# A step-ahead state space, two more projected blocks in front of z, and a shorter routing that issues its first gathers

## The chip, the cores and the metric

One core of one Trainium2 chip runs the whole program in one launch. The metric is the device time of that core in microseconds (us). The kernel before was timed three times: 1570.29, 1573.99 and 1575.91 us, median 1573.99. The engines are TensorE (PE; its weight loads are PEld), VectorE (DVE), ScalarE (ACT), GpSimd (POOL) and SyncE (SP), which here only issues DMAs.

## The reference

512 tokens of width 1024 pass through two transformer blocks, all in float32. Block 1, cut to what the change touches:

```python
proj = x @ w_in                          # q k v iq ik iw z xbc dt
q, k, iq, ik = rope(q), rope(k), rope(iq), rope(ik)
att = dsa_attention(q, k, v, iq, ik, iw) # index scores pick 128 keys a query, then softmax
xbc = silu(conv4(xbc)); dt = softplus(dt_raw + dt_bias)
y   = ssd_chunked(xs * dt, dt * a, B, C) # 4 chunks of 128 tokens, 8 heads, state 64x64
y   = rms((y + d_skip * xs) * silu(z)) * norm_w
x   = layer_norm(ALPHA * x + [att, y] @ w_out)
x   = layer_norm(ALPHA * x + moe(x))     # 16 experts in 4 groups, 2 of a token's best group
```

Inside `ssd_chunked`, a chunk gives three things: a diagonal part (C B^T masked by decays, times X), the chunk's own contribution to the state, and C times the state carried in from the chunks before. Block 2 has two other attention branches and a second `moe` with 32 experts, 2 a token. In both `moe`s a token's rows are gathered by expert, each expert has its own weights (3 MB), and the two results of a token are added with gates.

## The kernel before, in words

A product in "three passes" (L238 to L242) writes a float32 operand as a high part that the PE multiplies fast and a low remainder, and adds high x high, low x high and high x low. The high part is an ACT copy and the low one a subtraction on POOL. A projected block of 128 columns is 8 pieces (one for each 128 rows of `w_in`) of three matmuls over all 512 tokens.

`front` (L347) projects blocks in the order FIRST (ten), each turned by rope or convolved, then z in 8 steps over 4 token tiles. At its start POOL alone makes the low part of the first weight (L514) and of all eight pieces of x (L526). After the tenth block DVE has 16 rounds of top-k (L366 to L369: MAX8 and MATCH_REPLACE8) for two of the query tiles.

`state_space` (L903) works the four chunks and, between their steps, the five blocks of LATER (40 pieces, L240 to L242 with `ssd_main`). The order of each engine is written out by hand. PE's order a chunk is: products (L978, L984, after DVE took the chunk before), states (L990), segments (L999), pieces, diagonals (L1008), a rotation (L970). DVE per chunk: inputs X and Xd (L1174, L1175), masked products (L1178), the state (L1188 to L1199), skip (L1205), two masks MT (L1211), the carried part (L1216, L1218), then y (L1220, L1222). POOL: cumulated decays (L1059), low parts (L1064), and the three operations of rope (L1069 to L1074). After the last chunk come the four roots on ACT (L1161) and four normalisations on DVE (L1233, L1234).

`route` (L1769) turns the router's logits into lists: for each tile of an expert (96 rows in block 1, 64 in block 2) which tokens are in it. It is one long chain of small DVE instructions, each of which waits for the one before (`step`), with three places where PE sums or gathers (L1823, L1824, L1829). The SP queue meanwhile loads the first experts' weights. The next code block, `experts` (L1951) or `experts_moving` (L2213), blanks the two gather buffers on DVE (L2163, L2459), copies an index column (L2052, L2339) and gathers the first tile's rows with an indirect DMA from POOL (L2055, L2342). PE's first transpose and SP's next weight load (L1765, called with the slots `late`) wait for that gather's semaphore `x_in[0]`.

Between code blocks all engines meet at a barrier, which is how a stage's last engine sets the start of the next.

## Time and profile before

| what | us |
|---|---|
| median of three runs | 1573.99 |
| the profiled execution, its own time | 1573.33 |
| its span in the trace | 1571.2 |
| PE busy over the span | 1297.1 |
| DVE, ACT, POOL busy | 714.0, 447.4, 440.1 |

The profile page gives shares over the whole span, and the stages differ: where PE is nearly always busy in one, it stands still for most of another. So the table of stretches (busy time of each engine between two times, granted PE clock, DMA share) is the view to begin with, and then the instructions in order of time at the borders of the stages. A granted clock of 1.00 is 2.4 GHz and 0.50 is 1.2 GHz. Busy times of PE overlap a little from one matmul to the next, so the distance between two starts is the better price.

### The profile page before, as it was taken

The page shows a single profiled execution, that of the slowest core. Times are in us where ns is not written, and L with a number is a line of the kernel's source. Part 1 is how long each engine was busy: PE and PEld are TensorE (multiplying, and loading weights), DVE is VectorE, ACT ScalarE, POOL GpSimd, SP SyncE. Part 2 cuts the span into 40 slices and gives each one's busy share as a digit, 9 for nine tenths or more (in the row PEclk, how much of TensorE's full clock was granted, in tenths as well). Part 3 has the DMA queues.
Part 4 walks back from the last instruction along what each step waited for, and adds up shares of the span by engine and source line. Part 5 has one row for each costly group of instructions (what it writes and reads, how often), then busy time and mean ns, then how long its engine had stood idle before and what let it go on. Part 6 is the DMA issues. An engine that isn't in the chain of part 4 may idle for free. (4 is left out here: it accounts for less than half of the span.)

```text
span 1571.2 us, 20768 instructions
## 1 busy us (share of the span) xinstructions
PE 1297.1 (83%) x7632; PEld 1047.4 (67%) x7634; DVE 714.0 (45%) x1283; ACT 447.4 (28%) x964; POOL 440.1 (28%) x418
## 2 busy tenths in 40 slices
PE   6968789939999419889999999999798929977782
PEld 5757467838999319768989978788676815544441
DVE  2797684553443464753653637672233351111112
ACT  3532322213332124433342243423323201111110
POOL 6336410201110204202423324134244003322223
PEclk9989968958999758989999999999899859999996
DMA  6200170149996431300311312322131589999995
GB/s 252 96 3 12 71 251 30 41 175 354 384 372 249 133 115 49 132 1 6 107 68 68 107 46 91 110 81 81 36 104 52 215 319 375 385 385 392 400 361 179
DMA packets 64699, 262.71 MB, mean 167 GB/s; under 512 B 8276, under 2 KB 18132, under 8 KB 51808
## 3 DMA queue, kind: packets, MB, share of 16 engines
q1 hardware_dynamic: 53600, 234.25, 40.0%
q0 software_dynamic: 9216, 20.99, 4.1%
q10 hardware_dynamic: 1792, 6.29, 1.1%
q8 instruction: 53, 0.87, 0.2%
q14 instruction: 38, 0.31, 0.1%
HBM read 242.56 MB, written 29.43 MB: 173 GB/s over the span
## 5 line engine op out<-in xcount | busy, mean ns | idle before, releaser
L1693 POOL TENSOR_TENSOR block_w_lo<-block_w,block_w_hi 128x512 fp32r<-128x512 f32 x96 | 130.4, 1360 | 220.7 <-ACT block_w_hi L1671 220.7
L2377 PE MATMUL e_gu<-e_w,e_xT 128*64 128x256 f32 x1024 | 129.9, 411 | 35.5 <-DMA e_w<-in_gu 34.6
L2377 PEld LDWEIGHTS e_gu<-e_w,e_xT 128*64 128x64 f32 x1024 | 84.1, 148 | 72.0 <-issue 42.1
L240 PE MATMUL dil_bank<-block_w_hi,xT_hi 128*128 128x512 f32 x288 | 116.8, 406 | 4.3 <-PEq L768 4.3
L241 PE MATMUL dil_bank<-block_w_lo,xT_hi 128*128 128x512 f32 x288 | 114.9, 399 | 0.0
L242 PE MATMUL dil_bank<-block_w_hi,xT_lo 128*128 128x512 f32 x288 | 114.8, 399 | 0.0
L1671 ACT ACTIVATE block_w_hi<-block_w 128x512 fp32r<-128x512 f32 x96 | 60.4, 631 | 182.8 <-PE dil_bank L242 117.4
L2447 DVE TENSOR_TENSOR e_prod<-e_sg,e_gu 128x128 f32<-128x128 f32 x32 | 9.2, 288 | 165.1 <-ACT e_sg L2487 165.1
L240 PEld LDWEIGHTS dil_bank<-block_w_hi,xT_hi 128*128 128x128 f32 x288 | 77.6, 269 | 8.6 <-issue 4.7
L241 PEld LDWEIGHTS dil_bank<-block_w_lo,xT_hi 128*128 128x128 f32 x288 | 77.7, 270 | 4.1
L242 PEld LDWEIGHTS dil_bank<-block_w_hi,xT_lo 128*128 128x128 f32 x288 | 77.6, 269 | 4.2
L778 POOL TENSOR_TENSOR block_w_lo<-block_w,block_w_hi 128x512 fp32r<-128x512 f32 x20 | 24.8, 1270 | 157.6 <-ACT block_w_hi L851 157.6
L2950 DVE COPY dil_nat<-dil_bank 128x512 f32<-128x512 f32 x36 | 24.9, 691 | 87.2 <-PE dil_bank L242 85.9
L2401 PE MATMUL e_ybank<-e_w,e_hT 128*64 128x512 f32 x256 | 62.2, 604 | 0.4 <-issue 0.4
L2084 PE MATMUL e_gate<-e_xT,e_w 128*128 128x96 f32 x512 | 61.7, 280 | 0.7 <-DVE e_xT L2132 0.7
L2084 PEld LDWEIGHTS e_gate<-e_xT,e_w 128*128 128x128 f32 x512 | 60.3, 197 | 1.0 <-issue 1.0
L2084 PEld LDWEIGHTS e_up<-e_xT,e_w 128*128 128x128 f32 x512 | 59.5, 192 | 1.7
L2084 PE MATMUL e_up<-e_xT,e_w 128*128 128x96 f32 x512 | 59.3, 274 | 0.0
L260 PE MATMUL hT_bank<-consts,h_nat 128*128 128x128 f32 x32 | 6.2, 383 | 55.6 <-PEq L1543 55.6
L2487 ACT ACTIVATE e_sg<-e_gu 128x128 f32<-128x128 f32 x32 | 8.9, 277 | 150.9 <-PE e_gu L2377 150.9
L2146 DVE TENSOR_TENSOR xT_lo<-e_w,xT_hi 128x2048 fp32r<-128x2048 f32 x16 | 36.7, 2292 | 33.1 <-ACT xT_hi L2199 31.3
L240 PE MATMUL gates_bank<-block_w_hi,xT_hi 128*128 128x512 f32 x128 | 50.5, 395 | 1.0 <-PEq L768 1.0
(477 smaller groups left out, 3154.4 us busy)
## 6 DMA issues: line engine op xcount, KB each, us to landing
e_w<-in_gu SPq DMA_DIRECT2D x48, 2048.0 KB, 16.3
e_w<-in_dn SPq DMA_DIRECT2D x48, 1024.0 KB, 18.6
block_w<-in_w_dil SPq DMA_DIRECT2D x9, 2048.0 KB, 8.1
block_w<-in_w_out SPq DMA_DIRECT2D x4, 2048.0 KB, 8.9
block_w<-in_w_gates SPq DMA_DIRECT2D x4, 2048.0 KB, 11.1
slot_rows<-blank SPq DMA_DIRECT2D x12, 512.0 KB, 5.9
slot_rows<-e_y ACTq DMA_DIRECT2D x16, 384.0 KB
w_t<-in_w_in_t SPq DMA_DIRECT2D x10, 512.0 KB, 3.9
```

Of the source, the lines that this page charges most:

```text
L240: pe.matmul(out, lhs[0], rhs[0], start=first, stop=False)
L241: pe.matmul(out, lhs[0], rhs[1], start=False, stop=False)
L242: return pe.matmul(out, lhs[1], rhs[0], start=False, stop=last)
L778: pool.tensor_tensor(lo, w, hi.bitcast(F32), ALU.subtract)
L1671: act.activation(wh[:, j % RING, 0:width[i]], k.w[:, slot, c, 0:width[i]], ACT.Copy).then_inc(hi_ready, 1)
L1693: pool.tensor_tensor(wl[:, j % RING, 0:width[i]], k.w[:, (q0 + i) % 2, c, 0:width[i]], wh[:, j % RING, 0:width[i]].bitcast(F32), ALU.subtr ...
L2084: ins = pe.matmul(bank[b % 2][:, m * S:(m + 1) * S], w1[b][:, w:w + P], xT[b % 2][:, c * S:(c + 1) * S], start=(c == 0), stop=(c == KD - 1))
L2146: dve.tensor_tensor(w2_part(k.xl, b, 0), w2[b][:].rearrange("p (q n) -> p q n", q=4), w2_part(k.xh, b, 0).bitcast(F32), ALU.subtract).then ...
L2377: ins = pe.matmul(gubank[b % 2][g * S:(g + 1) * S, 0:2 * FG], xT[b % 2][:, c * S:(c + 1) * S], w1[b][:, w:w + 2 * FG], start=(c == 0), sto ...
L2401: ins = pe.matmul(bank[rows_of, :], hT[:, c * S:(c + 1) * S], w2[b][:, c * DM + m * 512:c * DM + (m + 1) * 512], start=(c == 0), stop=(c = ...
L2447: dve.tensor_tensor(prod[:], sg[:], gubank[b % 2][0:U, FG:2 * FG], ALU.mult).then_inc(prod_ready, 1)
L2950: return dve.tensor_copy(nat[:, i, tt, :], bank[:, 0:512])
```

## The change

In `front`, blocks 4 and 0 move from LATER to FIRST, so twelve blocks are projected in front of z and three remain in the state space. Their rope is done there by ACT and POOL (`late_rope`) between z's steps. At the start, the low part of the first weight and of the odd pieces of x is made on DVE, the rest on POOL.

In `state_space`, the diagonal, states and products are put in another order: DVE makes the next chunk's inputs and masked products before it takes the y of this chunk, PE computes the next chunk's products while this one's diagonals run, and the carried part is read earlier. The squares of three chunks get one root and one reciprocal, and the last its own. The SP load of the fifth block goes.

In `route`, pairs of DVE instructions are joined, ranks over token tiles are summed by PE in bfloat16 (eight matmuls), the thresholds (5 in block 1, 7 in block 2) are compared in one instruction with a sum behind it, the gates are moved behind the list of tokens, and the first half of the gathering matmuls may start a token choice earlier. POOL blanks the gather buffers in `route` and issues the first two gathers there as soon as `tok_of` is written; the experts' block then starts at the third.

```diff
-FIRST = (14, 7, 5, 6, 8, 9, 10, 11, 12, 13)
-LATER = (4, 0, 1, 2, 3)
+FIRST = (14, 7, 5, 6, 8, 9, 10, 11, 12, 13, 4, 0)
+LATER = (1, 2, 3)
@@ front
+                def late_rope(i):
+                    r = ROPED + i
+                    o = k.ropeT[:, FIRST[LATE0 + i], :]
+                    pool.wait_ge(raw_ready, r + 1)
+                    pool.tensor_tensor(o, raw[:, r % 2, :], k.c("cos"), ALU.mult).then_inc(cos_done, 1)
+                    pool.wait_ge(turn_ready, i + 1)
+                    pool.tensor_tensor(relu[:, r % 2, :], relu[:, r % 2, :], k.c("sin"), ALU.mult).then_inc(sin_done, 1)
...
-                split_w(0)
-                for c in range(KD):
+                for c in range(0, KD, 2):
                     pool.wait_ge(xh_ready, c + 1)
...
+                dve.wait_ge(wh_ready, 1)
+                dve.tensor_tensor(w_l[:, 0], w_t[:, 0], w_h[:, 0].bitcast(F32), ALU.subtract).then_inc(first_low, 1)
+                for c in range(1, KD, 2):
+                    dve.wait_ge(xh_ready, c + 1)
+                    dve.tensor_tensor(k.xl[:, c], xT[:, c], k.xh[:, c].bitcast(F32), ALU.subtract).then_inc(xl_ready[1], 1)
@@ state_space, PE's order from the first chunk to the third
                 products(0)
+                states(0)
                 segment(0)
                 segment(1)
                 pieces(0, 4)
+                products(1)
+                pieces(4, 5)
                 diagonal(0)
-                pieces(4, 8)
+                pieces(5, 6)
                 diagonal(1)
-                products(1)
                 segment(2)
-                rotate(0)
-                pieces(8, 10)
                 segment(3)
+                states(1)
+                pieces(6, 8)
+                products(2)
...
@@ state_space, DVE
+                inputs(0)
+                masked(0)
                 for c in range(TT):
                     if c < TT - 1:
+                        state(c)
...
+                    if c < TT - 1:
+                        inputs(c + 1)
+                        masked(c + 1)
...
                     dve.wait_ge(ydiag_done, 2 * (c + 1))
                     dve.tensor_tensor(y2[:], y1[:], b_y[:], ALU.add).then_inc(y_free, 1)
@@ route
+                for x in k.xg:
+                    pool.memset(x[:], 0.0).then_inc(xg_ready, 1)
+                pool.wait_ge(k.rows_stored, 16 * TT)
+                pool.wait_ge(xg_ready, 2)
+                pool.wait_ge(tok_ready, 1)
+                for b in range(2):
+                    pool.indirect_dma_start(k.xg[b][:], None, rows, bass.IndirectOffsetOnAxis(
+                        ap=k.tok_of[:, b:b + 1], axis=0), bounds_check=SEQ - 1, oob_is_err=False).then_inc(x_in[b], 16)
...
+                for tt in range(TT):
+                    pe.matmul(totals[:, 0:E], ones[:], M[:, tt, :], start=(tt == 0), stop=(tt == TT - 1))
+                pe.matmul(rbank[:, 0:TT * E], before[:], flat, start=True, stop=False)
+                for tt in range(1, TT):
+                    ins = pe.matmul(rbank[:, tt * E:TT * E], ones[:], flat[:, 0:(TT - tt) * E], start=False, stop=(tt == TT - 1))
...
+                step(dve.tensor_tensor(above[:], bc(totals[:, 0:E], 2, J), bc(full[:], 1, E), ALU.is_gt))
+                step(dve.reduce_sum(extra[:], above[:], AX))
@@ experts, experts_moving
-                for x in xg:
-                    dve.memset(x[:], 0.0).then_inc(blank, 1)
```

## Rows read from the trace of the kernel before

**Rows 1.** Stretches: length, busy us (instructions) by engine, PEclk, DMA share, GB/s.
```profile
20.50:105.00 84.50, 84.40 (x376) 64.97 (x376) 64.14 (x122) 38.69 (x68) 35.70 (x19) 1.00 0.27 94
...
116.30:187.20 70.90, 55.78 (x298) 44.45 (x298) 48.45 (x67) 21.43 (x37) 45.74 (x28) 0.93 0.03 8
187.20:327.20 140.00, 125.67 (x654) 99.19 (x656) 81.98 (x155) 38.63 (x102) 20.20 (x16) 0.82 0.32 114
...
355.40:520.00 164.60, 163.81 (x1294) 151.82 (x1295) 66.04 (x90) 54.01 (x67) 16.26 (x28) 0.98 0.86 326
...
1288.80:1535.00 246.20, 210.59 (x1521) 119.92 (x1521) 31.46 (x94) 40.05 (x94) 69.71 (x119) 0.94 0.99 378
```
**Rows 2.** Order of time (start, us, engine, line) at the start of `front`.
```profile
5.82 2.34 POOL L514 TENSOR_TENSOR w_t_lo<-w_t,w_t_hi 128x1024 fp32r<-128x1024 f32 x1 [5.38 <-ACT w_t_hi L544]
9.35 8.80 POOL L526 TENSOR_TENSOR xT_lo<-block_w,xT_hi 128x512 fp32r<-128x512 f32 x7
20.53 0.50 PE L240 MATMUL proj_main<-xT_hi,w_t_hi 128*128 128x512 f32 x1 [1.35 <-POOL w_t_lo L514]
```
**Rows 3.** Order of time, a projection's matmuls and the end of `front`.
```profile
21.33 0.39 PE L240 MATMUL proj_main<-xT_hi,w_t_hi 128*128 128x512 f32 x1
21.56 0.40 PE L241 MATMUL proj_main<-xT_lo,w_t_hi 128*128 128x512 f32 x1
...
102.90 2.66 ACT L627 ACTIVATE z<-proj_main 128x512 f32<-128x512 f32 x4
...
115.14 0.69 DVE L373 TENSOR_SCALAR key_bias<-score 128x256 bf16<-128x256 f32 x2
```
**Rows 4.** DVE groups by line in 116.3 to 187.2: busy us, mean ns, idle before.
```profile
L1211 DVE TENSOR_TENSOR ssd_mt<-ssd_l,ssd_gm 128x512 f32<-128x512 f32 x8 | 13.1, 1664 | 0.8 <-ACT ssd_l L1101 0.6
L1220 DVE TENSOR_TENSOR ssd_y<-ssd_y,ssd_ydiag 128x512 f32<-128x512 f32 x4 | 2.7, 687 | 9.7 <-PE ssd_ydiag L1008 9.7
L1233 DVE RECIPROCAL ssd_ms<-ssd_ms 128x1 f32<-128x1 f32 x4 | 0.7, 163 | 5.1 <-ACT ssd_ms L1161 5.0
```
**Rows 5.** Order of time in the second chunk, and the stage's last instruction.
```profile
137.16 2.82 POOL L1064 TENSOR_TENSOR block_w_lo<-block_w,block_w_hi 128x1024 fp32r<-128x1024 f32 x1
137.78 4.20 DVE L1211 TENSOR_TENSOR ssd_mt<-ssd_l,ssd_gm 128x512 f32<-128x512 f32 x2
177.13 1.29 POOL L1074 TENSOR_TENSOR ropeT<-ropeT,x_res 128x512 f32<-128x512 f32 x1
185.96 0.75 DVE L1234 SCALAR_TENSOR_TENSOR ssd_y<-ssd_y,ssd_ms,ssd_vec 128x512 f32<-128x512 f32 x1
```
**Rows 6.** Order of time in block 1's `route`.
```profile
335.66 0.80 DVE L1896 SCALAR_TENSOR_TENSOR r_extra<-r_counts,r_extra 128x16 f32<-128x16 f32 x4
340.61 0.56 DVE L1917 TENSOR_TENSOR r_ohr<-consts,r_r 128x384 f32<-128x384 f32 x1
343.01 2.76 PE L1829 MATMUL r_tbank<-r_ohj,r_ohr 128*96 128x26 f32 x16 [9.72 <-DVE r_ohj L1920]
345.89 0.18 DVE L1933 TENSOR_SCALAR r_tok_of<-r_tbank 96x26 uint32<-96x26 f32 x1 [1.59 <-PE r_tbank L1829]
```
**Rows 7.** Order of time, block 1's first gather and the weight load behind it.
```profile
351.08 1.16 POOL L2055 DMA_INDIRECT e_xg<-token_rows,e_idx  x1 [1.02 <-issue]
355.38 0.34 SPq L1765 DMA_DIRECT2D e_w<-in_gu  x1
```
**Rows 8.** Landing of the 48 gathers; DMA in two stretches.
```profile
DMA to landing us min/median/max: 3.8/10.5/12.0
...
344.00:348.00 4.00, 1.78 (x12) 1.65 (x11) 0.70 (x4) 0.00 (x0) 0.00 (x0) 0.50 0.04 16
...
1284.00:1286.00 2.00, 0.00 (x0) 0.00 (x0) 0.45 (x1) 0.00 (x0) 0.48 (x2) 0.50 0.71 295
```
**Rows 9.** Order of time, block 2's token list and its next load.
```profile
1280.08 0.20 DVE L1933 TENSOR_SCALAR r_tok_of<-r_tbank 64x48 uint32<-64x48 f32 x1
1288.77 0.33 SPq L1765 DMA_DIRECT2D e_w<-in_gu  x1
```

More of the change, by code:

```diff
@@ L351, in front @@
     NB, CONV0 = len(FIRST), 1 + ROPED
+    LATE0 = CONV0 + CONV_BLOCKS
     TAKEN, FLOOR, ROUNDS = -3.0e38, -1.0e35, TOPK // 8
@@ L1130, in square, with roots @@
                         act.wait_ge(squared, c)
-                    act.activation(yy[:], k.y[:, c, :], ACT.Square, accum_out=ms[:, c, 2:3]).then_inc(squared, 1)
+                    act.activation(yy[:], k.y[:, c, :], ACT.Square, accum_out=ms[:, 0, c:c + 1]).then_inc(squared, 1)
+                def roots(first, end):
+                    act.activation(ms[:, 2, first:end], ms[:, 1, first:end], ACT.Sqrt).then_inc(rms_ready, 1)
                 split_high(0)
@@ new lines, in state @@
+                def state(c):
+                    dve.wait_ge(st_done, c + 1)
+                    s3 = St[:].rearrange("p (h d) -> p h d", h=4)
+                    if c >= 1:
+                        for g in range(2):
+                            r = slice(HD * g, HD * (g + 1))
+                            step(dve.tensor_tensor(s3[r], s3[r], bc(decay[r, 1, c * 8 + 4 * g:c * 8 + 4 * g + 4], 2, HD),
+                                                   ALU.mult))
+                    for g in range(2):
+                        r = slice(HD * g, HD * (g + 1))
+                        if c >= 1:
+                            ins = dve.tensor_tensor(St[r, :], St[r, :], b_st[r, g * HW:(g + 1) * HW], ALU.add)
+                        else:
+                            ins = dve.tensor_copy(St[r, :], b_st[r, g * HW:(g + 1) * HW])
+                        if g == 0:
+                            step(ins)
+                    ins.then_inc(st_ready, 1)
@@ L1782, in route @@
     k.exp_of = k.sb(ctx, f"{name}_exp_of", [1, NT - E], I32)
+    k.xg = [k.sb(ctx, f"{name}_xg{i}", [S, DM]) for i in range(2)]
     k.used = k.sb(ctx, f"{name}_used", [1, 1], I32)
@@ L1792, in route @@
         picked = k.sb(s, f"{name}_picked", [P, 2, TT, E])
-        M = k.sb(s, f"{name}_m", [P, TT, E])
-        extra, cum, base, zero, counts = (k.sb(s, f"{name}_{n}", [P, E]) for n in ("extra", "cum", "base", "zero",
-                                                                                  "counts"))
-        rank = k.sb(s, f"{name}_rank", [P, TT, E])
+        M, ones, before = (k.sb(s, f"{name}_{n}", shape, BF16) for n, shape in (("m", [P, TT, E]), ("ones", [P, P]),
+                                                                              ("before", [P, P])))
+        full = k.sb(s, f"{name}_full", [P, J])
+        above = k.sb(s, f"{name}_above", [P, E, J])
+        past = k.sb(s, f"{name}_past", [P, 2, TT, J])
+        extra, cum, base, zero = (k.sb(s, f"{name}_{n}", [P, E]) for n in ("extra", "cum", "base", "zero"))
         cmp = k.sb(s, f"{name}_cmp", [1, NT - E, E])
@@ L1834, in _ @@
             def _(act):
+                act.activation(ones[:], k.c("ones"), ACT.Copy).then_inc(bits_ready, 1)
+                act.activation(before[:], k.c("before"), ACT.Copy).then_inc(bits_ready, 1)
+                act.activation(full[:], k.c("iota")[:, 1:J + 1], ACT.Copy, scale=float(S)).then_inc(bits_ready, 1)
                 act.wait_ge(diff_ready, 1)
@@ L1904, in _ @@
                 step(dve.reduce_sum(tile[:], picked[:], AX))
-                step(dve.tensor_scalar(over[:], pos[:], S - 0.5, None, ALU.is_gt))
-                q_now = over
-                for j in range(2, -(-SEQ // S)):
-                    step(dve.scalar_tensor_tensor(q[:], pos[:], j * S - 0.5, q_now[:], ALU.is_gt, ALU.add))
-                    q_now = q
+                step(dve.tensor_tensor(past[:].rearrange("p i t j -> p (i t) j"), bc(pos[:].rearrange("p i t -> p (i t)"), 2, J),
+                                       bc(full[:], 1, 2 * TT), ALU.is_ge))
@@ L1911, in _ @@
+                step(dve.reduce_sum(q[:], past[:], AX))
+                step(dve.tensor_scalar(over[:], q[:], 1.0, None, ALU.min))
                 step(dve.tensor_tensor(tile[:], tile[:], own[:], ALU.subtract))
                 step(dve.tensor_tensor(tile[:], tile[:], over[:], ALU.mult))
+                step(dve.tensor_tensor(own[:], own[:], q[:], ALU.add))
                 step(dve.tensor_tensor(tile[:], tile[:], own[:], ALU.add))
-                step(dve.tensor_tensor(tile[:], tile[:], q[:], ALU.add))
@@ L1959, in experts @@
     with ExitStack() as s:
-        xg = [k.sb(s, f"{name}_xg{i}", [S, DM]) for i in range(2)]
+        xg = k.xg
         idx = [k.sb(s, f"{name}_idx{i}", [S, 1], U32) for i in range(2)]
@@ L2226, in experts_moving @@
     with ExitStack() as s:
-        xg = [k.sb(s, f"{name}_xg{i}", [S, DM]) for i in range(2)]
+        xg = k.xg
         idx = [k.sb(s, f"{name}_idx{i}", [S, 1], U32) for i in range(2)]
```

365 lines of the change are left out of this document (176 added, 189 removed).

## The prediction

> **What bounds the kernel now.** I read the table of stretches first. It shows three kinds of stage that the change touches [rows 1]. From 20.5 to 105 PE is busy 84.4 of 84.5 us: that part of `front` is PE's. From 116.3 to 187.2 (the state space) PE has 55.8 of 70.9, DVE 48.5 and POOL 45.7: three engines share the bound, so a gain on one is cut short by the next. The experts of block 1 are PE's (163.8 of 164.6), those of block 2 are the DMA's (share 0.99 over 246 us). Both shift rigidly with the moment at which they begin, and they begin with the landing of a gather. Second, the order of time at the four borders: the start of `front` [rows 2], its end [rows 3], the list of tokens [rows 6] and the first gather [rows 7, 9]. Third, the groups of the state space [rows 4, 5], where the idle time before an instruction and its mean against its shortest say who waits.
>
> **Start of `front`.** POOL starts the first low part of w at 5.82 and takes 2.34, then eight pieces of x at 8.80/7 = 1.26, then the second w; PE can start its second block at 20.53 and waited 1.35 for it [rows 2]. In the new code DVE makes the first w: two halves of about 0.6 (a DVE operation of 512 columns is recorded with 0.69 [rows 4]), done at 7.0. The x pieces alternate, four of 1.26 on POOL and four of 0.69 on DVE. Do they run beside each other? The masks MT say no: two that should take 1.4 took 4.20 while POOL had a 2.82 us subtraction and another after it [rows 5]. So the eight pieces take 4 x 1.95 = 7.8, to 14.8; POOL's second w takes 2.34, to 17.2. PE's first block keeps up with this (its last piece comes at 14.8 and takes 0.7). The start comes 3.3 earlier (2 if ACT's high parts are late, 5 if the two engines do not block each other).
>
> The Trainium skill, page SBUF — State Buffer, "Who interferes with whom", says that a DVE instruction with two SBUF inputs and a GpSimd one that reads SBUF exclude each other for a whole instruction. The row above agrees. Had it not held, the x pieces would end at 12.0 and the start would come 5 earlier.
>
> **Rest of `front`.** PE gets 2 blocks x 24 matmuls x 0.23 (start to start in [rows 3]) = 11.1, and two rotations, which I price with their neighbours at 1.5 together (0.9 to 2.5; no row of mine shows one alone). The last silu of z ended at 102.90 + 2.66 = 105.56 [rows 3]. It now ends at 105.56 - 3.3 + 12.6 = 114.9. DVE's top-k rounds set the end before: 115.14 + 0.69 = 115.83 [rows 3]; they move with the start, to 112.5. So this stage gains only 0.9: DVE had covered 10.3 us of PE's idle time and the two new blocks fill it. ACT and POOL have room: both are busy under half of the stretch [rows 1], and POOL's six new rope operations (1.29 each [rows 5]) lie between low parts of z that PE needs every 2.8 us (12 x 0.23). Range of the stage: 2 lost to 2 gained. DMAs: the same blocks load, one SP issue less later; no queue is passed.
>
> **State space.** Removed: 16 pieces, 16 x 0.70 = 11.2 of PE, two rotations, two low parts (2.34) and six rope operations on POOL: its work falls from 8 x 1.0 + 5 x 2.34 + 15 x 1.29 = 39 to 26.6. DVE loses no work but waits: the eight MTs cost 1.664 on average against 0.69, so 7.8 us are blocked time [rows 4]; with two thirds of POOL's work left some 2.6 of these go, and about as much on its other two-input operations. DVE also stood 9.7 before L1220 (it waits for the diagonals) and 5.1 before the roots came back [rows 4]. The new order puts the next chunk's inputs into the first, and one root for three chunks ahead of the last y shortens the second to 1 or 2.
>
> To join these I walked both written orders, each engine taking its next instruction when its semaphores allow it, with the durations of the trace and DVE's two-input operations and POOL's excluding each other. For the order of before it gives 71.1; measured are 186.71 - 116.3 = 70.4 [rows 5]. For the new order DVE's y2 of the four chunks comes at 13.7, 26.4, 40.4 and 48.9 and the last POOL rope at 57.4, DVE at 56.2. **I take 57.4, a gain of 13.4** (rounded down from 13.7). Bounds: 50 if POOL hardly blocks (DVE 48.5 less 5, plus its first waits), 62 if each chunk keeps DVE's chain of 12.4 (the present period of 14.3 less 1.6 of waiting and its gaps) and the clock costs 2. What is late next is POOL: it ends the stage with three ropes behind one another. PE now idles up to 3.8 us at a time; its clock is at 0.93 in this stage [rows 1].
>
> **Route, block 1.** A small dependent step costs 0.80/4 = 0.20 [rows 6]. From the ranks to the first `ohr` the chain ran to 340.61. New chain: ranks are ready about 333.6 (eight bfloat16 matmuls for four float32 entries; 333.3 to 334.3), thresholds and their sum 0.55, scan and base 0.44, four instructions of 128 columns 1.28, `past` and its sum 0.44, eight small ones 1.6: 337.9. Two choices of 0.3 + 0.3 + 0.56 [rows 6]: 340.2. PE's first half runs under the second choice, so its second half, 1.4 of 2.76 [rows 6], ends at 341.7, and `tok_of` at 341.9 against 345.89 + 0.18 = 346.07: 4.2 earlier. The six gate steps (1.2) move behind it and delay nothing that the gather needs. Then the gather itself: before, 5.0 lay between `tok_of` and the issue at 351.08 (barrier, two blankings, an index copy), 4.30 from issue to SP's next load [rows 7]. Now the issue follows in about 1.0 (its own "issue" time in [rows 7]), at 342.9; landing at 347.2. POOL's second issue ends about 345.9 and the barrier costs 1.5, so the experts start at 347.4 against 355.4. **Gain 8.0.** The weights have landed by then: DMA share is 0.04 from 344 [rows 8]. POOL's blanking and semaphore clears have 14 us of cover; without it at most 3. Bounds 5 to 10.
>
> **Route, block 2.** Same counts with 32 experts: I get 1276.2 for `tok_of` against 1280.28 [rows 9]; issue at 1277.1. But here three experts' weights are still arriving, to about 1285.3 (share 0.71 in 1284 to 1286 [rows 8]). Gathers took 3.8 to 12.0, median 10.5 [rows 8], so this one lands between 1281 and 1287. The stage behind is DMA-bound, so what counts is only the gap between 1285.3 and 1288.8, the load that SP issues at the landing [rows 9]: 3.5 at most, 1.5 at least. I take **2.5**.
>
> The Trainium skill, page DMA: Bandwidth & Descriptors, "SWDGE vs HWDGE vs iDMA", says that each DMA engine goes round its queues in turn, hardware and software ones. By that a gather is not held until the weights are in, and the gain is the whole gap, 3.5; the median of 10.5 speaks for less. It moves the sum by 1.
>
> **Sum.** 0.9 + 13.4 + 8.0 + 2.5 = 24.8. Against the profiled execution's own 1573.33 that is 1548.5; it lies within 1 us of the median of the runs, so no correction.
>
> **Rivals.**
> *Gathers wait for the queue.* Issued into running weight loads they land 12 us later instead of 4.3 [rows 8]: block 1 then starts at 354.9 and gains 0.5, block 2 gains 0. Sum 14.8: 1558.5. Against it: block 1's loads end at 344.
> *DVE's chain stays the bound of the state space* at 62 or more, and `front` ends 1 later: gain 8 - 1 + 10.5 = 17.5, 1556.
> *More than forecast:* the state space at 53, whole gap in block 2, a warmer PE in the stages behind (187 to 327 ran at 0.82 [rows 1]): 31, 1542.
> *Slower than before:* PE has 55.8 - 11.2 - 2 = 43 us of work in a stage of 57, and long pauses bring the clock to 0.5, as in 344 to 348 [rows 8]. If it stays there for the whole stage the work is 86 us, 28 more than the forecast's 57.4: 24.8 of gain turn into a loss of 3.8, 1577. It decides from 25 us of added PE time. Against: most of its pauses are under 4 us.
> *The change does not do what it says:* order and waits leave the stages as they were, 1573, within 0.3%.
>
> **Chances.** Forecast 0.62 (its own range 1543 to 1554), queue 0.10, chain 0.13, more 0.08, slower 0.03, nothing 0.04. The range 1540 to 1561 leaves out under 2 in 10. This kernel's runs lie 5.6 apart, so 0.3% (4.7 us) is about what can be told from no change. Faster 0.93, same 0.04, slower 0.03.
>
> **What would show it.** PE's second block starts near 17.2; z's last silu and not a top-k round ends `front`, near 115; the state space lasts 55 to 60 and its last instruction is POOL's rope; MT's mean falls below 1.4; the first indirect DMA starts near 343 in block 1 and near 1277 in block 2, and both stand before the barrier; the experts' stages last as long as before. I am wrong if an expert stage lengthens by what its start gains, or if the clock row of the state space falls well under 0.93.

## The result, and the profile after

The changed kernel takes 1554.86 us (median of four runs, 1552.74 to 1559.26), the kernel before 1574.87. The ratio is 0.9894, 95% interval 0.9860 to 0.9928: faster by 11 to 22 us. The forecast was 1548.5 in a range of 1540 to 1561. The profiled execution of the changed kernel is its slowest, 1559.26 with a span of 1557.2.

First the table of stretches of the changed kernel: length, busy us (instructions) of PE, PEld, DVE, ACT and POOL, PEclk, DMA share, GB/s. It answers to [rows 1].

```profile
16.10:105.00 88.90, 88.90 (x390) 68.35 (x389) 68.09 (x134) 41.02 (x67) 46.79 (x27) 1.00 0.28 98
114.40:176.40 62.00, 47.01 (x246) 37.11 (x246) 46.65 (x63) 16.84 (x29) 29.59 (x20) 0.87 0.00 1
176.40:315.80 139.40, 122.79 (x656) 96.77 (x656) 81.69 (x155) 38.63 (x102) 20.19 (x16) 0.84 0.32 114
337.90:502.50 164.60, 163.90 (x1290) 151.90 (x1291) 66.15 (x90) 53.41 (x66) 16.24 (x28) 0.98 0.87 325
1275.00:1520.60 245.60, 211.03 (x1521) 119.37 (x1523) 31.22 (x94) 39.70 (x94) 69.54 (x118) 0.94 0.99 378
```

The state space went from 70.9 to 62.0. The stages that the change does not touch kept their lengths (139.4, 164.6, 245.6). One stretch differs that the table shows only in part: from block 1's first expert tile to block 2's route it took 904.2 before and 907.8 after. But for the place of the first two gathers, its code is the same in all 13 kernels profiled here, and its length follows the mean granted clock in it, from 907.8 at 0.925 (the changed kernel) to 894.0 at 0.941 (e6). That is why the stages below are compared, and not only the totals.

The table gives, for every kernel of this study, what its profile says of the stages. "No drain" means that the barrier at the end of `route` does not wait for GpSimd's own DMAs (e1). State space: first `ssd_go` matmul to attention's first. Tile 1 and tile 2: start of the first transpose of an expert's tile (`e_xbank`) behind the route's first instruction (`r_zero`), block 1 and block 2. MB: what the DMAs moved in the first 60 us of block 2's route (its GB/s times 60). Last: start of PE's last group of `e_gu` matmuls behind block 2's route start. The ratio stands to the kernel before on the same chip; the chips differ (the kernel before took 1565.3 beside e11 and 1574.9 beside the changed kernel), so totals are to be compared by the ratio and not by the median.

| kernel | state space | tile 1 | tile 2 | MB | last | median us | ratio (95%) |
|---|---|---|---|---|---|---|---|
| before | 70.9 | 28.2 | 29.2 | 21.6 | 275.3 | 1574.9 | |
| after | 62.0 | 22.0 | 29.3 | 21.5 | 274.9 | 1554.9 | 0.9894 (0.9860 to 0.9928) |
| e1 no drain | 60.8 | 19.3 | 25.9 | 22.4 | 272.4 | 1548.5 | 0.9853 (0.9822 to 0.9883) |
| e2 gathers back | 61.8 | 24.3 | 28.6 | 21.7 | 275.2 | 1553.0 | 0.9881 (0.9848 to 0.9913) |
| e3 route only | 70.9 | 22.2 | 29.1 | 21.8 | 275.3 | 1569.8 | 0.9986 (0.9965 to 1.0007) |
| e4 front, state space | 63.0 | 28.0 | 29.1 | 21.6 | 274.2 | 1559.1 | 0.9915 (0.9881 to 0.9949) |
| e5 warm | 57.8 | 22.0 | 28.9 | 21.8 | 274.4 | 1551.1 | 0.9879 (0.9841 to 0.9918) |
| e6 states early | 56.4 | 22.0 | 29.0 | 21.8 | 274.6 | 1547.1 | 0.9858 (0.9820 to 0.9895) |
| e7 four slots, no drain | 62.4 | 19.5 | 20.3 | 22.0 | 273.9 | 1547.2 | 0.9850 (0.9811 to 0.9889) |
| e8 gather between loads | 62.0 | 19.5 | 26.0 | 22.2 | 273.6 | 1551.7 | 0.9879 (0.9838 to 0.9920) |
| e9 no drain, states early | 55.4 | 19.4 | 25.8 | 22.5 | 272.1 | 1544.5 | 0.9830 (0.9795 to 0.9865) |
| e10 all three | 56.0 | 19.4 | 26.0 | 22.4 | 273.0 | 1542.9 | 0.9830 (0.9787 to 0.9872) |
| e11 six slots | 62.1 | 22.2 | 29.2 | 21.6 | 274.4 | 1547.8 | 0.9881 (0.9847 to 0.9914) |

**Front.** Order of time in the changed kernel (start, us, engine, line, operation, tiles), as in [rows 2, 3]:

```profile
5.74 1.22 DVE L708 TENSOR_TENSOR w_t_lo<-w_t,w_t_hi 128x1024 fp32r<-128x1024 f32 x1 [4.59 <-ACT w_t_hi L575]
7.11 6.67 DVE L711 TENSOR_TENSOR xT_lo<-block_w,xT_hi 128x512 fp32r<-128x512 f32 x4
...
13.19 2.84 POOL L531 TENSOR_TENSOR w_t_lo<-w_t,w_t_hi 128x1024 fp32r<-128x1024 f32 x1
...
111.00 0.69 DVE L374 TENSOR_SCALAR key_bias<-score 128x256 bf16<-128x256 f32 x2
...
111.47 2.66 ACT L666 ACTIVATE z<-proj_main 128x512 f32<-128x512 f32 x4
```

POOL's second low part ends at 16.03 (forecast 17.2), z's last silu at 114.13, behind the last top-k round at 111.69. The state space starts at 114.43 against 116.37: 1.9 us.

**State space.** DVE's groups (busy us, mean ns, idle before), as in [rows 4]:

```profile
L1268 DVE TENSOR_TENSOR ssd_mt<-ssd_l,ssd_gm 128x512 f32<-128x512 f32 x8 | 8.8, 1132 | 1.6 <-ACT ssd_l L1140 1.5
...
L1227 DVE TENSOR_TENSOR ssd_state<-ssd_state,ssd_decay 64x256 f32<-64x256 f32 x4 | 4.1, 1022 | 3.5 <-PE ssd_st L1032 3.4
...
L1277 DVE TENSOR_TENSOR ssd_y<-ssd_y,ssd_ydiag 128x512 f32<-128x512 f32 x4 | 2.8, 688 | 5.6 <-PE ssd_ydiag L1050 5.6
```

The masks fell from 1.664 to 1.132 on average, the wait for the diagonals from 9.7 to 5.6, the one for the roots from 5.0 to nothing. New is a wait of 3.4 for `states` (L1032). The longest wait of PE's matmuls there (engine, line, releaser: us in total, times, longest):

```profile
PE ssd_go L1019 <- DVE ssd_y L1256: 6.7, 2, 4.1
```

A stand is a time in which PE has nothing to do. It has three here: 2.6 us up to 117.50, 2.6 up to 136.8, and 4.1 up to 153.4. PE's granted clock about them is the third number from the end:

```profile
117.00:120.00 3.00, 2.50 (x7) 2.14 (x8) 1.32 (x4) 0.71 (x1) 2.65 (x1) 0.50 0.02 5
120.00:123.00 3.00, 3.00 (x16) 3.00 (x15) 2.06 (x4) 0.60 (x1) 1.04 (x1) 0.50 0.00 0
135.00:138.00 3.00, 1.18 (x8) 0.89 (x8) 2.87 (x5) 1.67 (x3) 1.84 (x1) 0.82 0.00 0
138.00:141.00 3.00, 3.00 (x11) 1.89 (x8) 2.96 (x3) 0.00 (x0) 2.22 (x2) 0.61 0.00 0
153.00:156.00 3.00, 2.63 (x12) 1.82 (x13) 2.90 (x5) 0.00 (x0) 0.00 (x0) 0.66 0.00 0
156.00:159.00 3.00, 3.00 (x17) 2.56 (x15) 1.18 (x3) 0.60 (x1) 0.94 (x1) 0.77 0.00 0
```

0.50 is the 1.2 GHz level, 1.00 the 2.4 GHz one. From 123 to 135 and from 141 to 153 the clock is 0.99 and 1.00 on average.

**Routes.** Order of time in both, as in [rows 6, 7, 9]:

```profile
329.41 0.18 DVE L1989 TENSOR_SCALAR r_tok_of<-r_tbank 96x26 uint32<-96x26 f32 x1 [0.51 <-PE r_tbank L1901]
...
330.63 1.14 POOL L1882 DMA_INDIRECT r_xg<-token_rows,r_tok_of  x1 [10.19 <-issue]
332.07 0.96 POOL L1882 DMA_INDIRECT r_xg<-token_rows,r_tok_of  x1 [0.31 <-issue]
...
337.55 0.34 SPq L1820 DMA_DIRECT2D e_w<-in_gu  x1
...
1262.36 1.01 POOL L1882 DMA_INDIRECT r_xg<-token_rows,r_tok_of  x1 [9.69 <-DVE r_tok_of L1989]
1263.67 0.95 POOL L1882 DMA_INDIRECT r_xg<-token_rows,r_tok_of  x1 [0.30 <-issue]
...
1274.64 0.33 SPq L1820 DMA_DIRECT2D e_w<-in_gu  x1
...
1275.01 1.08 PE L2424 MATMUL e_xbank<-consts,r_xg 64*128 64x64 f32 x8 [14.73 <-PEq L1866]
```

In block 1 the first gather is issued 14.7 us behind the route's start in place of 23.8, 9.0 earlier, but SP's next load comes only 6.4 earlier (PE's first tile 6.2): 6.9 us lie between issue and load, where before it were 4.3 [rows 7]. In block 2 the issue is 9.3 earlier (16.7 against 26.0) and the experts start at 29.3 against 29.2: nothing. PE's wait there is not for a DMA but for L1866, which is `with nc.Block() as block` of `route`: its closing barrier. DVE had done its last at 1263.30 and POOL its second issue at 1264.62.

### The profile page after: what moved, and what is told of

It is laid out like the page before. It is cut to its first block and busy times, and to the rows that moved or that the text cites. A ratio compares the mean times of both kernels' runs of the same rounds, so it can differ in the third digit from the quotient of the medians.

```text
span 1557.2 us, 20719 instructions
## 1 busy us (share of the span) xinstructions
PE 1300.1 (83%) x7642; PEld 1049.4 (67%) x7642; DVE 710.7 (46%) x1248; ACT 448.6 (29%) x968; POOL 430.3 (28%) x413
## 5 line engine op out<-in xcount | busy, mean ns | idle before, releaser
L822 POOL TENSOR_TENSOR block_w_lo<-block_w,block_w_hi 128x512 fp32r<-128x512 f32 x20 | 24.8, 1272 | 155.9 <-ACT block_w_hi L895 155.9
L2144 PEld LDWEIGHTS e_gate<-e_xT,e_w 128*128 128x128 f32 x512 | 60.8, 198 | 1.0 <-issue 1.0
L2768 POOL TENSOR_TENSOR block_w_lo<-block_w,block_w_hi 128x384 fp32r<-128x384 f32 (+2 forms) x28 | 29.2, 1048 | 79.6 <-ACT block_w_hi L2781 79.6
## 6 DMA issues: line engine op xcount, KB each, us to landing
e_w<-in_gu SPq DMA_DIRECT2D x48, 2048.0 KB, 14.7
```

The source lines that it names most:

```text
L822: pool.tensor_tensor(lo, w, hi.bitcast(F32), ALU.subtract)
L2144: ins = pe.matmul(bank[b % 2][:, m * S:(m + 1) * S], w1[b][:, w:w + P], xT[b % 2][:, c * S:(c + 1) * S], start=(c == 0), stop=(c == KD - 1))
L2768: pool.tensor_tensor(wl[:, j % RING, 0:width[i]], k.w[:, (first_chunk + i) % 2, c, 0:width[i]], wh[:, j % RING, 0:width[i]].bitcast(F32), ...
```

## The experiments

**e1: the closing barrier.** What does the barrier wait for? The DMA records of the changed kernel point at the two gathers. The last packets of the software queue, which here carries GpSimd's gathers, end at 336.00 in block 1 and at 1273.11 in block 2, and SP's next loads come 1.5 us behind each, at 337.55 and 1274.64. So the wait for GpSimd's own DMAs, the drain, is taken out of the barrier, in `route` alone:

```diff
-        with nc.Block() as block:
+        with nc.Block(no_gpsimd_drain=True) as block:
```

> The changed kernel, with one edit in route: its block closes without waiting until GpSimd's own DMAs are done (no_gpsimd_drain=True), everything else stays. In the changed kernel SP loaded again only at 337.55 and TensorE turned its first tile at 337.89, although the second gather was issued at 333.03 and no DMA moved data after 336. Theory A, the closing barrier waits for both gathers to end: without it, block 1's route ends some 1.5 us after the second issue (about 334.5), TensorE then waits for the first gather alone and starts 1.5 to 2.5 us earlier (335.5 to 336.5, where the route starts at 315.8); in block 2 the engines leave the block at about 1266 in place of 1274.5 and wait for the first gather itself, which the weight queue holds up: 0 to 1.5 us there. Together 1.5 to 4 us less. Theory B, the gathers' own landing sets both starts: engines leave the block earlier, but SP's load and TensorE's first transpose stay 21.8 and 13.8 us behind the route's start: 0 us.

Order of time in this kernel, both routes, and its DMAs in the first 60 us of block 2's route:

```profile
327.58 1.14 POOL L1882 DMA_INDIRECT r_xg<-token_rows,r_tok_of  x1 [10.17 <-issue]
...
332.18 1.51 PE L2135 MATMUL e_xbank<-consts,r_xg 96*128 96x96 f32 x8 [5.92 <-DMA r_xg<-token_rows,r_tok_of]
...
1253.20 1.01 POOL L1882 DMA_INDIRECT r_xg<-token_rows,r_tok_of  x1 [9.70 <-DVE r_tok_of L1989]
...
1262.43 1.08 PE L2424 MATMUL e_xbank<-consts,r_xg 64*128 64x64 f32 x8 [11.30 <-DMA r_xg<-token_rows,r_tok_of]
...
1236.50:1296.50 60.00, 36.00 (x285) 21.58 (x285) 20.80 (x79) 9.01 (x21) 14.02 (x22) 0.73 0.98 374
```

PE now waits for the gather by name, and SP loads again at 1262.31, before the gathers' last packet at 1264.06. Block 1 starts 4.6 us behind the issue in place of 7.3 (2.7 less), block 2 9.2 in place of 12.7 (3.4 less). Theory A, and by more than its numbers (1.5 to 2.5 in block 1, 0 to 1.5 in block 2). By stages the barrier had cost 5.2 us: 2.7 in block 1 and 2.5 at the last group of block 2. The median is 6.3 lower, 1548.54, but in the profiles 1.2 of that is a state space of 60.8 in place of 62.0, which the edit does not touch, and the intervals of the two ratios overlap a little.

**e2: the early issue alone.** The first two gathers and the blanking of their tiles go back to the experts' block (the short routing stays):

```diff
 route:
-                for x in k.xg:
-                    pool.memset(x[:], 0.0).then_inc(xg_ready, 1)
...
-                for b in range(2):
-                    pool.indirect_dma_start(k.xg[b][:], ...).then_inc(x_in[b], 16)
 experts, now for the first two tiles as well:
                     pool.tensor_copy(idx[b % 2][:], k.tok_of[:, bass.ds(t, 1)]).then_inc(idx_ready, 1)
...
+                for x in xg:
+                    dve.memset(x[:], 0.0).then_inc(blank, 1)
```

> The changed kernel with the first two gathers (index copy, issue) and the blanking of their tiles back in the experts' block, as before; the shorter routing stays. Prices the early issue alone. Theory A (the gathers inside route are worth the code between tok_of and the issue, less what the closing barrier now waits for): block 1's experts start 3 to 4 us later than in the changed kernel (about 341 for a route start at 315.8), block 2's 1 to 3 us later: 4 to 7 us more in all. Theory B (the barrier gives all of it back): under 1.5 us more. Block 2: if its gather is held by the weights' queue alone, an issue some 9 us later still lands behind the same weights, and its start moves by less than 2 us.

Order of time, block 2:

```profile
1263.87 1.03 POOL L2396 DMA_INDIRECT e_xg<-token_rows,e_idx  x1 [0.92 <-POOL e_idx L2393]
...
1270.20 1.09 PE L2422 MATMUL e_xbank<-consts,e_xg 64*128 64x64 f32 x8 [14.00 <-DMA e_xg<-token_rows,e_idx]
```

Block 1 starts 2.3 later than in the changed kernel. Block 2, issued 5.6 us later, starts 0.7 earlier: 6.3 us from issue to use. Block 2's last group comes 0.3 later. So by stages the early issue is worth 2.6 us, between theory B (under 1.5) and theory A (4 to 7), and the total shows nothing of it (ratio 0.9881 against 0.9894). It is nearer to theory B: the barrier gives most of it back. In block 1, 3.9 of the 6.2 us that the route won are thus the shorter chain, and 2.3 the early gathers.

**e3 and e4: the parts apart.** e3 is the kernel before with the new `route` and experts; e4 the kernel before with the new `front` and `state_space`:

```diff
 e3: -def route(k, name, E, G, S, lg, ctx, loads, retired):
     +def route(k, name, E, G, S, lg, ctx, loads, retired, rows, x_in):      # and what it holds; front, state_space of before
 e4: +                inputs(0)                                              # and all of front and state_space; route of before
     +                masked(0)
```

> The kernel before with the change's part in route and the experts alone; front and state space as before. By the two traces the routes gave 6.4 us in block 1 and 0.1 in block 2: theory A (parts add up) 6.5 us less than before, so about 1568. The forecast's 10.5 us for both routes would give 1564. If the gain hangs on the earlier parts (clock of later stages, other order), under 4 us.

> The kernel before with the change's part in the front and the state space alone; route and experts as before. By the two traces the front gave 2.0 us and the state space 8.9, attention 0.6: theory A (parts add up) 11 us less than before, about 1563.5; the forecast had 14.3 us for both. If the clock in stages behind takes some back, 7 to 10 us.

By stages the parts stand as in the whole: e3 has a tile 1 of 22.2 and a tile 2 of 29.1, e4 a state space of 63.0. By time e4 is 13.2 us under the kernel before (expected were 11). e3 is only 2.4 under it; by its interval it is between 5.5 us faster and 1.1 slower, which leaves out the expected 6.5. How much of this is the clock can be seen in runs of equal mean clock. At 0.903 and 0.904 e3 took 1567.2 to 1568.7 and the kernel before 1569.6 to 1573.2, some 3 us more, and e4 took 1558.1 to 1561.8, some 11 us less than the kernel before. So e4 is theory A, and of e3's 4 missing us the clock explains about 1. The other 3 or so stay open: e3's tile 1 comes 6.0 earlier in its profile, and no view shows where that is lost.

**e5: keep PE busy.** 36 bfloat16 matmuls, whose result is overwritten, in the three places where PE stands, the last of them behind a new wait for `turn_ready`:

```diff
                 products(0)
+                keep_warm(10)
                 states(0)
...
+                keep_warm(10)
                 products(2)
...
+                pe.wait_ge(turn_ready, 1)
+                keep_warm(16)
                 products(3)
```

> The changed kernel with 36 extra bfloat16 matmuls (128 x 512, into a bank whose result is overwritten later) in the state space, in the places where TensorE stands: 10 behind products(0), 10 ahead of products(2), 16 ahead of products(3). In the changed kernel its stands of 2.6, 2.6 and 4.1 us stood beside a granted clock of 0.50 in 117 to 123, 0.61 to 0.82 in 135 to 141 and 0.66 to 0.77 in 153 to 159. Theory A (the clock lost there is the reason why the state space took 62.0 us and not 57.4): with no stand the granted clock stays near 1.00 and the stage takes 57.5 to 59.5. Theory B (the order of the work and DVE's and POOL's interference make the 62): clock up, stage still 61 to 63, or longer where an extra matmul delays the next product.

The whole stage, then the three stretches that were slow in the changed kernel:

```profile
113.80:171.70 57.90, 48.91 (x281) 35.92 (x284) 47.59 (x63) 16.90 (x30) 30.47 (x20) 0.97 0.00 1
117.00:123.00 6.00, 6.00 (x38) 5.07 (x40) 5.17 (x8) 1.31 (x3) 6.00 (x4) 1.00 0.00 0
135.00:141.00 6.00, 4.50 (x33) 3.84 (x32) 5.53 (x9) 0.00 (x0) 1.90 (x2) 1.00 0.01 3
153.00:159.00 6.00, 6.00 (x39) 5.07 (x39) 4.49 (x10) 2.49 (x6) 1.74 (x2) 1.00 0.00 0
```

Clock 1.00 in all three, the stage 57.8 where the same work without the extra matmuls took 60.8 to 63.0 in seven profiles. Theory A: work that computes nothing made the stage 4.2 us shorter than in the changed kernel. The totals (ratios 0.9879 and 0.9894) do not tell the two apart.

Could it be the places of the extra matmuls, and not the clock? e1 answers that. It has the changed kernel's state space, without them, but in its profile the clock stayed at 1.00 for the first 24 us. The same 24 us of e1 and of e5, each with the DVE group of the fourth mask:

```profile
113.70:137.70 24.00, 17.33 (x109) 13.98 (x110) 20.94 (x25) 7.94 (x11) 17.33 (x10) 1.00 0.00 1
135.66 2.25 DVE L1268 TENSOR_TENSOR ssd_mt<-ssd_l,ssd_gm 128x512 f32<-128x512 f32 x2
...
113.80:137.80 24.00, 21.50 (x127) 15.74 (x129) 20.92 (x25) 7.94 (x11) 17.36 (x10) 1.00 0.00 1
135.78 2.27 DVE L1276 TENSOR_TENSOR ssd_mt<-ssd_l,ssd_gm 128x512 f32<-128x512 f32 x2
```

The fourth mask ends 24.2 us behind the stage's start in both, and 26.9 behind it in the changed kernel, whose clock is 0.83 on average there. Up to that point the extra matmuls did nothing but keep the clock. Behind it e1's clock falls twice, and it loses 1.6 us to e5 by the sixth mask and 1.4 more by the eighth; the 9.4 us from there to the stage's end are equal again. The mean clock alone does not order the seven profiles, though: e7 has 0.91 and takes 62.4, the changed kernel has 0.87 and takes 62.0. Nor is a loss at one place kept in full: at the fourth mask the changed kernel is 2.7 us behind e1, at the end of the stage 1.2.

**e6: the order on PE.** DVE's wait of 3.4 for `states` comes from PE's order, in which two segments and a rotation stand ahead of it:

```diff
                 diagonal(1)
+                states(1)
                 segment(2)
                 segment(3)
-                states(1)
...
                 diagonal(3)
+                states(2)
                 segment(4)
                 segment(5)
                 rotate(0)
-                states(2)
```

> The changed kernel, and in TensorE's order of the state space states(1) and states(2) stand right behind diagonal(1) and diagonal(3), ahead of the segments and of rotate(0). DVE waited 1.29 and 2.15 us for them in the changed kernel. Theory A (the order on TensorE holds up DVE's state step, and through it off_free and TensorE's own next products): the two waits fall below 0.5 us, TensorE's stands ahead of products(2) and (3) shorten from 2.6 and 4.1 to under 2 and 3, and the stage takes 58.5 to 60.5 in place of 62.0. Theory B (DVE's wait is only moved: the segments come later, so exp and MT do): 61.5 to 62.5, with the wait now at MT.

The stage's stretch, then its waits:

```profile
114.20:170.70 56.50, 43.17 (x248) 34.23 (x248) 47.68 (x63) 17.03 (x30) 30.93 (x20) 0.96 0.00 1
```

```profile
DVE ssd_y L1277 <- PE ssd_ydiag L1050: 3.3, 2, 2.1
...
DVE ssd_mt L1268 <- ACT ssd_l L1140: 1.4, 2, 0.8
...
PE ssd_go L1019 <- DVE ssd_y L1256: 1.5, 1, 1.5
```

The wait for `states` (3.4 at L1227) is gone, PE's wait for DVE fell from 6.7 to 1.5, the masks' wait for ACT's exp stayed (1.5, now 1.4). With shorter stands fewer falls of the clock are left: one near the stage's start, and one in its last 2 us. 56.4 is better than theory A's 58.5 to 60.5, which had not counted the clock. The profile is of this kernel's fastest run by far (1534.07 at clock 0.921; its other six are 1546.07 to 1550.24), so its total says little; e9 repeats the stage.

**e7 and e8: what holds block 2's gather.** Both without the drain. e7 queues 6 MB of weights ahead of the gathers (as block 1 does) and the next only when the first has landed; e8 queues them as soon as both gathers are issued:

```diff
 e7: -              lambda sp: first_loads(sp, weights, range(2, SLOTS_2 - 1), ...)      # late: range(SLOTS_2 - 1, SLOTS_2)
     +              lambda sp: first_loads(sp, weights, range(2, 4), ...)                # late: range(4, SLOTS_2)
 e8: as e7, in route:
     +                pool.sem_inc(issued, 1)            # behind the two gathers
     +                    sp.wait_ge(issued, 1)
     +                    after_issue(sp)                # slots 4 and 5
```

> The kernel without GpSimd's drain at the block's end (as in the run before), and block 2's route loads two slots of weights (2 and 3) in place of three; slots 4 and 5 are loaded once the first gather has landed. Asks what holds block 2's gather: there it landed about 9.0 us after its issue, with 9 MB of weights queued at the route's start, and in block 1 about 4.5, with 6 MB. Theory A (the weights ahead in the queues hold it): it lands 4 to 5 us after its issue, and TensorE's first tile starts 21 to 22 us behind the route's start, in place of 25.9. Theory B (something else, such as 64 rows or the issue itself): 25 to 26. It asks as well what sets the end: from the first tile to the end's last e_gu group it was 245.1 to 246.6 us in six profiles. Theory C (the start of the experts carries through): the end comes 4 us earlier, about 1544.5. Theory D (the stream of weights carries through, and it now stands idle 4 to 6 us): the end comes 3 to 5 us later, about 1552.

> As the run without the drain, and in block 2's route SP loads slots 2 and 3, waits until GpSimd has issued both gathers, and then loads slots 4 and 5 in the same block. The gathers stand ahead of 6 MB of weights, and the stream stands for 2 to 4 us. Theory A (the queue holds the gather): first tile 21 to 22.5 us behind the route's start. Theory B (the DMA engines share themselves between queues whatever the order): 24 to 26. With the start carried through (theory C), about 1544.5; with the stream (theory D), 1549 to 1551.

Order of time in e7, and its DMAs in the first 60 us:

```profile
1256.30 1.01 POOL L1882 DMA_INDIRECT r_xg<-token_rows,r_tok_of  x1 [9.69 <-DVE r_tok_of L1989]
...
1259.92 0.87 PE L2424 MATMUL e_xbank<-consts,r_xg 64*128 64x64 f32 x6 [5.70 <-DMA r_xg<-token_rows,r_tok_of]
...
1239.60:1299.60 60.00, 41.61 (x329) 25.09 (x331) 21.80 (x82) 10.28 (x24) 15.74 (x25) 0.77 0.96 366
```

and in e8:

```profile
1249.26 1.01 POOL L1886 DMA_INDIRECT r_xg<-token_rows,r_tok_of  x1 [9.68 <-DVE r_tok_of L1994]
...
1249.61 0.33 SPq L1820 DMA_DIRECT2D e_w<-in_gu  x1
...
1258.59 0.66 PE L2429 MATMUL e_xbank<-consts,r_xg 64*128 64x64 f32 x4 [11.40 <-DMA r_xg<-token_rows,r_tok_of]
```

In e7 the gather is there 3.6 us after its issue: theory A. In e8 it takes 9.3, as much as in e1 (9.2), though the new weights were issued 0.35 us behind it and the old ones ended within 2 us, as in e7 (whose DMA share is 0.35 from 18 to 21 us behind the route's start): theory B there. So the gather need not stand behind the weights to be late; weight loads that come after it make it as late.

The records of the software queue's packets (both gathers together, 160 packets) show how. In e7 they begin 1.7 us behind the first issue and last 2.2 us. In e8 they begin at 2.8 and last 8.6, and in e1, with weights queued ahead, they begin at 4.4 and last 6.5. As to the end: e7 starts its experts 5.6 us earlier than e1 and ends 1.5 later. Neither C nor D as written, and its median, 1547.19, is not to be told from e1's; the MB rank the two ends (22.0 against 22.4).

The Trainium skill, page "DMA: Bandwidth & Descriptors", section "Queues, rings and completion order", says that a DMA's semaphore increment lands only after every earlier write of that DMA engine, across its queues, and that an engine goes round its queues packet by packet. The drawn-out packets of e8 agree with the second: the gather began among the weights and was served among them. How much the first adds no run here tells, since the records do not say which packets are the first gather's.

**e9 and e10: together.** e9 is e1's and e6's edit, e10 has e5's matmuls as well.

> The changed kernel with both edits that helped: no wait for GpSimd's own DMAs at the end of route's block, and states(1), states(2) ahead of the segments in TensorE's order. Theory A (the parts add up): state space 56.4 as in the profile of the run with the early states, routes as in the run without the drain (first tiles 19.3 and 25.9 behind the routes' starts), together 10 to 12 us less than the changed kernel: 1543 to 1545. Theory B (that profile was of a run with an unusually high clock, 0.921 where its other six were 0.904 to 0.910, and its granted clock dipped only once in the state space): here the granted clock dips again behind TensorE's stands, the stage takes 58 to 60.5, and the whole is 1545 to 1548.

> The run before it with the 36 extra bfloat16 matmuls in TensorE's stands as well (10 behind products(0), 10 ahead of products(2), 16 ahead of products(3)). Theory A (clock and order are two causes of the 62.0, and add): granted clock 1.00 throughout, DVE's waits for states under 0.5 us, state space 54.5 to 56.5, and the whole 1541 to 1545. Theory B (they are one cause: with the early states the stands are short, and the extra matmuls, 36 of 0.21 us, then stand on TensorE's path): 57 to 59, no better than the run without them.

The state space in e9:

```profile
113.90:169.30 55.40, 43.10 (x248) 33.96 (x248) 47.70 (x63) 16.97 (x30) 31.71 (x20) 0.97 0.00 1
```

and in e10:

```profile
113.90:169.90 56.00, 49.32 (x282) 35.81 (x283) 48.60 (x63) 16.80 (x30) 31.41 (x20) 0.97 0.01 1
```

DVE's masks in e9 (busy us, mean ns), and one pair of them in order of time:

```profile
L1268 DVE TENSOR_TENSOR ssd_mt<-ssd_l,ssd_gm 128x512 f32<-128x512 f32 x8 | 11.7, 1501 | 0.1
...
133.20 4.45 DVE L1268 TENSOR_TENSOR ssd_mt<-ssd_l,ssd_gm 128x512 f32<-128x512 f32 x2
```

e9: theory A, 1544.5, some 10 us under the changed kernel, and the stage of 56.4 was no luck. e10 fits neither theory whole: 56.0 lies in A's range (54.5 to 56.5) and not in B's (57 to 59), but it is no better than e9's 55.4, as B said. It could hardly be better: in e9's profile the clock was at 1.00 for the first 45 us even without the extra matmuls, so they had little to keep. What the runs do show is that clock and order both count. With the clock at 1.00 nearly throughout, the old order takes 57.8 (e5) and the new one 56.0 (e10): 1.8 us for the order. With the old order, the changed kernel takes 62.0 and e5 57.8: 4.2 for the clock. The new order wins most of the second sum too (56.4, 55.4), since with it PE's stands are shorter. DVE is now the busiest engine, 47.7 of 55.4 us. e10's total, 1542.85, cannot be told from e9's. e9 is the version to keep: its ratio to the kernel before is 0.983 (0.9795 to 0.9865), against the change's 0.989 (0.9860 to 0.9928).

**e11: the queues' standstill.** The changed kernel, with the fourth slot queued too:

```diff
-        route(..., lambda sp: first_loads(sp, weights, range(2, SLOTS_2 - 1), ...)
+        route(..., lambda sp: first_loads(sp, weights, range(2, SLOTS_2), ...)                 # late: none
```

> The changed kernel (with the wait for GpSimd's own DMAs at the block's end), and block 2's route queues all four remaining slots of weights, 2 to 5, in place of 2 to 4: the DMA queues do not run dry while the engines wait at the block's end (in the changed kernel they stood for about 1.9 us from 27 us behind the route's start). Asks what carries through to block 2's end, measured from the route's start to TensorE's last e_gu group: 274.9 in the changed kernel, 272.4 without the drain (start of the experts 25.9, no standstill of the queues), 273.9 with four slots and no drain (start 20.3, standstill about 2.3). Theory C (the start of the experts carries through): start unchanged at 29.3 or later, last group at 274.5 to 275.5. Theory D (the stream of weights carries through): start 29 to 31, last group at 272 to 273.2, some 2 us less in all. If the longer queue holds the second gather, the start moves to 33 or later, and the end by it under theory C.

Start 29.2, last group 274.4: by the numbers set down, close to theory C (274.5 to 275.5) and outside theory D (272 to 273.2). But the standstill is not gone, it moved. Two stretches of e11, the old place (27 to 31 us behind the route's start) and the new one (35 to 37):

```profile
1259.00:1263.00 4.00, 1.11 (x10) 0.98 (x10) 0.42 (x1) 0.53 (x2) 0.18 (x1) 0.50 1.04 440
...
1267.00:1269.00 2.00, 1.95 (x21) 1.23 (x17) 0.33 (x2) 0.32 (x2) 0.01 (x1) 1.00 0.28 76
```

By 35 all that was queued is loaded, and SP's next load comes only at 36.3, behind the first tile, which the barrier held to 29.2. So the run did not make the case it was meant to make.

What sets the end is seen over all 13 kernels. Each moves the same 94.9 MB on SP's queue from the route's start to PE's last `e_gu` group, and from 60 us on the DMAs move 385 or 386 GB/s with a share of 1.00 or 1.01 in every one. What is left to differ is how much was moved in the first 60 us, and that puts the end in order: 21.5 to 21.8 MB go with 274.2 to 275.3, 22.0 and 22.2 with 273.9 and 273.6, 22.4 and 22.5 with 273.0 to 272.1. On average 21.7 MB go with 274.8 (eight kernels) and 22.5 MB with 272.5 (three): 0.8 MB at the stage's 378 GB/s are 2.1 us, and the ends differ by 2.3. The stream carries through to the end; the experts' start does only where it frees a slot sooner. No run changes the stream alone, so this rests on the comparison of the profiles.

## Why the forecast was near, and which steps failed

In the range, 6.4 us too low, and just outside the 1543 to 1554 that the forecast gave as its own; of the rivals, the one at 1556 is nearest. The steps against the profile (us gained):

| step | forecast | measured |
|---|---|---|
| front | 0.9 | 1.9 |
| state space | 13.4 | 8.8 |
| route, block 1 | 8.0 | 6.2 |
| route, block 2, to the last group | 2.5 | 0.4 |
| the rest (attention +0.6, tail -0.5) | 0 | 0.2 |
| sum | 24.8 | 17.5 |

17.5 from 1573.33 is 1555.8, 0.9 from the measured median; the profiled run's other 3.6 lie in the middle stages, whose length follows the clock. The total is near because the large terms have the right sign and roughly the right size. Three were too high and only `front` too low, so hardly anything of it is errors that cancel. But one of the prediction's own signs of being wrong came: the clock row of the state space fell from 0.93 to 0.87.

*Front: right in kind.* PE's second block could start 1.1 earlier than forecast, because DVE's and POOL's low parts held each other up less: a pair of x pieces took 1.67 us (6.67 for four) and not the 1.95 of one behind the other, so all eight were there at 13.8 and not at 14.8. z's silu sets the end, as said.

*State space: the term that was mis-sized.* The mechanism came as forecast: MT's mean under 1.4, the roots' wait gone, POOL's rope last (it ends at 176.11). The length of 57.4 came from a walk in which each PE operation kept the duration it has at full clock, although the new order leaves PE idle for up to 3.8 us at a time; the text saw the pauses and gave the danger 0.03, as one that would have to last the whole stage. It did not have to: about stands of 2.6 to 4.1 us PE ran several us with the clock at or near 0.50, and the states and diagonals that DVE waits for came later. e5, which keeps the clock up, gives 57.8, 0.4 from the forecast. So the walk was near to right at full clock, and the term that it lacked is 4.2 us of clock. The number of 62 is also that of the rival "DVE's chain stays the bound", without its reason: it was PE's clock, and the order of PE's work is worth another 1.8 at full clock.

*Route, block 1: chain right, barrier wrong.* `tok_of` came 5.0 earlier (forecast 4.2), the issue 9.0 (8.2). The step "the barrier costs 1.5" failed: from POOL's second issue to the experts' start it is 4.9 us, and 2.2 in e1, because the barrier waits for the DMAs that the new code issues inside the block. That is why the early gathers are worth 2.3 in block 1 and next to nothing in block 2 (e2). The rival "gathers wait for the queue" does not hold here: 4.6 us in e1.

*Route, block 2: wrong.* The forecast took 2.5 us from the gap in the stream of weights, 0.4 came. The gap stayed, because SP stood at the barrier: the DMA share over the first 60 us is 0.93 before and 0.94 after. The rival "gathers wait for the queue" was half right: beside weight loads the gather does take 9 us (e1, e8). But the larger error was in the order of thought. The stream starts with the route, whatever the route's length, and sets the end. A shorter route can give back only the time for which the stream stands still, and the changed kernel had moved 21.5 MB after 60 us, the kernel before 21.6.

## What to carry to other kernels

Before moving a software DMA ahead of a block's end, look at what the closing barrier waits for: an engine's wait put down to the `Block` line itself, and not to a tile, is the sign. When a stage is no longer bound by PE, price its matmuls at the clock that the trace shows about PE's own stands, and put in front, in PE's order, what another engine's chain is waiting for. Where a stage is bound by a stream of loads, ask when the stream starts and where it stands, and not how long the code beside it is.

## What the runs showed of the hardware

- PE does nothing in the state space for 2.6 us from 0.5 us behind the stage's start in nine profiles, those of the changed kernel, e1, e2, e4, e6 to e9 and e11. In seven the granted clock fell to 0.50 about it (in the changed kernel from 1.00 in `front` to 0.50 in 117 to 123); in e1 and e9 it stayed at 1.00. So the same stand can cost the clock or not, and one profile does not tell. In the kernel before PE had stood for 11.4 us ahead of the stage, and the clock was 0.50 in its first 6 us.
- An indirect gather of 64 rows was in use 3.6 us after its issue with the queues nearly empty, 6.3 in e2, where it was issued 5.6 us later into the weight loads' last part, and 9.2 to 9.3 beside weight loads, whether these were issued before it or after it.
- A barrier at a block's end with the drain let SP go on 1.5 us after the last packet of the gathers issued inside it, in both routes of the changed kernel.
- The masks' mean rose again with the shorter stands, from 1.13 us in the changed kernel to 1.26 in e5 and 1.50 in e9 (eight of them, 11.7 us). In the slowest pair, 4.45 us from 133.20, POOL has a subtraction of 2.52 from 132.88 and a rope product of 1.73 behind it. A pair alone takes 1.4. So with clock and order mended DVE and POOL hold each other up more. Whether the next gain in this stage lies there is not tested.
